# Three context k-tiles of each joint norm move from GpSimd to VectorE, and norm operations increment their readers' semaphores themselves

## The reference, cut to what matters

```python
def rms_norm_2(x, w):
    xf = x.astype(jnp.float32)
    y = xf * lax.rsqrt(jnp.mean(xf * xf, axis=-1, keepdims=True) + NORM_EPS)
    return (y * w.astype(jnp.float32)).astype(x.dtype)

def modulate(h, shift, scale):
    return h * (1.0 + scale) + shift
```

## Time and profile before

| | |
|---|---|
| median of 3 runs | 3286.22 us (3282.61 to 3289.34) |
| profiled execution, its time | 3286.13 us |
| its span, first to last instruction | 3284.1 us |
| PE busy | 3086.7 us (94%), 19874 matmuls |
| DVE busy | 1655.5 us (50%), 2636 instructions |
| ACT busy | 1155.5 us (35%), 1824 instructions |
| POOL busy | 574.0 us (17%), 500 instructions |
| mean granted TensorE clock | 0.976 |

### The profile page before, as it was taken

One profiled execution on the slowest core, in us unless ns is written; L12 is line 12 of the kernel. 1 busy time (PEld: TensorE's weight loads), 2 busy tenths in 40 slices (PEclk: granted clock), 3 DMA queues, 4 the chain that ended last, 5 costly groups with the idle time before them and its releaser, 6 DMA issues. The chain is left out here.

```text
span 3284.1 us, 49467 instructions
## 1 busy us (share of the span) xinstructions
PE 3086.7 (94%) x19874; PEld 2476.7 (75%) x19874; DVE 1655.5 (50%) x2636; ACT 1155.5 (35%) x1824; POOL 574.0 (17%) x500
## 2 busy tenths in 40 slices
PE   7988999999989999998988899999989999899998
PEld 5666766877657888776777788888868888678886
DVE  5643587455246664335663332332367877643332
ACT  4211354543123222344774311111254544432221
POOL 0000022011023441141552200000043233100000
PEclk9999999999989999998999999999989999899999
DMA  3466111223312222301000102112131121122222
GB/s 136 174 250 260 58 74 64 77 77 127 117 38 92 78 103 89 111 14 65 2 2 27 52 33 97 52 39 90 34 109 59 59 78 59 70 91 77 103 89 79
DMA packets 34146, 271.00 MB, mean 83 GB/s; under 512 B 3200, under 2 KB 5760, under 8 KB 14720
## 3 DMA queue, kind: packets, MB, share of 16 engines
q1 hardware_dynamic: 33920, 267.85, 22.6%
HBM read 263.64 MB, written 4.19 MB: 82 GB/s over the span
## 5 line engine op out<-in xcount | busy, mean ns | idle before, releaser
L751 PE MATMUL banks<-normed_high,weights_high 128*128 128x512 f32 (+1 forms) x2168 | 802.3, 378 | 27.7 <-DVEq L544 9.1
L751 PE MATMUL banks<-normed_low,weights_high 128*128 128x512 f32 (+1 forms) x2168 | 789.7, 373 | 0.0
L418 ACT ACTIVATE weights_high<-ring 128x1024 fp32r<-128x1024 f32 (+2 forms) x335 | 339.8, 1014 | 1010.4 <-PE banks L751 762.8
L308 DVE TENSOR_TENSOR weights_low<-ring,weights_high 128x1024 fp32r<-128x1024 f32 (+2 forms) x281 | 329.0, 1171 | 724.0 <-ACTq L420 706.9
L751 PEld LDWEIGHTS banks<-normed_high,weights_high 128*128 128x128 f32 x2168 | 411.8, 190 | 118.4 <-issue 17.3
L751 PE MATMUL banks<-normed_high,weights_low 128*128 128x512 f32 (+1 forms) x2168 | 497.9, 371 | 1.4 <-DVEq L440 1.4
L751 PEld LDWEIGHTS banks<-normed_low,weights_high 128*128 128x128 f32 x2168 | 411.7, 190 | 78.6 <-issue 4.6
L751 PEld LDWEIGHTS banks<-normed_high,weights_low 128*128 128x128 f32 x2168 | 380.9, 189 | 77.8 <-DVEq L440 2.3
L685 POOL TENSOR_TENSOR latent_total<-latent_total,latent_square 128x512 f32<-128x512 f32 x42 | 62.6, 1491 | 1185.3 <-ACTq L664 1185.3
L751 PE MATMUL banks<-ffn_hidden_high,weights_high 128*128 128x512 f32 (+1 forms) x704 | 251.3, 366 | 0.0
L751 PE MATMUL banks<-ffn_hidden_low,weights_high 128*128 128x512 f32 (+1 forms) x704 | 251.1, 366 | 0.0
(11 more groups left out here) (618 smaller groups left out, 4835.6 us busy)
## 6 DMA issues: line engine op xcount, KB each, us to landing
ring<-in_ada SPq DMA_DIRECT2D x48, 1024.0 KB, 6.4
ring<-in_ffn_up SPq DMA_DIRECT2D x22, 2048.0 KB, 8.1
ring<-in_hgrn SPq DMA_DIRECT2D x16, 1536.0 KB, 6.3
ring<-in_ffn_down SPq DMA_DIRECT2D x16, 1408.0 KB, 6.0
ring<-in_gates SPq DMA_DIRECT2D x6, 2048.0 KB, 8.1
ring<-in_wo SPq DMA_DIRECT2D x6, 2048.0 KB, 8.1
ring<-in_ffn_up2a SPq DMA_DIRECT2D x4, 2048.0 KB, 8.1
ring<-in_ffn_up2b SPq DMA_DIRECT2D x4, 2048.0 KB, 8.0
```

Source lines behind the costliest of these rows:

```text
L308: e.eng.tensor_tensor(out, x, hi.bitcast(F32), ALU.subtract).then_inc(e.sem, e.tick())
L418: e.eng.activation(self.by_k(k.WH), self.source(), ACT.Copy).then_inc(e.sem, e.tick())
L751: mm = pe.matmul(ps[:, 0:y.shape[-1]], w, y, start=(kk == 0 and n == 0), stop=(kk == kt - 1 and n == len(every) - 1))
```

## The change

The context norms of `q2`, `ffn_up2a` and `hgrn` get `rest=5` and a `partner`, the latent norm of the same place. GpSimd makes context k-tiles 0 to 4. VectorE makes 5 to 7 in a new loop, `by_rest`, behind its latent norm, in the partner's `scaled` buffers, with two operations a k-tile; ScalarE's roundings keep their order. PE waits for them through `wait_ready`. Norm operations now increment their reader's semaphore themselves; the waits for the engine's own counter and the separate increments are gone, except one inside GpSimd between L540 and L308. `scaled` has three buffers where there is room (`w_rw`, `wk`, `ffn_up2a`, `hgrn`), with a wait for the low part that last read the buffer. In `ffn_up`, `ffn_up3` and `q2` it stays at two. The unsplit norms and `Rounded` are changed alike. In `hgrn`, `clear_keys` waits for five context k-tiles of GpSimd instead of eight.

```diff
@@ class Normed
+    def wait_ready(self, eng, t):
+        c, n = self.ready_at(t)
+        eng.wait_ge(c.sem, c.at(n + 1))
...
     def by_scalar_rounding(self, e, t):
+        if t >= self.rest:
+            n = t - self.rest
+            x = self.partner.scaled[n % len(self.partner.scaled)][:, 0:self.width]
+            e.eng.wait_ge(self.rest_made.sem, self.rest_made.at(n + 1))
+            e.eng.activation(self.dst(t)[0], x, ACT.Identity, bias=self.shift(t)).then_inc(self.rest_rounded.sem, 1)
+            return
...
-            e.eng.activation(hi, x, ACT.Identity, bias=self.shift(t), scale=gain).then_inc(e.sem, e.tick())
-        e.eng.wait_ge(e.sem, e.now())
-        e.eng.sem_inc(self.rounded.sem, 1)
+            e.eng.activation(hi, x, ACT.Identity, bias=self.shift(t), scale=gain).then_inc(self.rounded.sem, 1)
+
+    def by_rest(self, e):
+
+        v, left, depth = e.eng, DT - self.rest, len(self.partner.scaled)
+        v.wait_ge(self.rooted.sem, self.rooted.at(1))
+        for n in range(left + 1):
+            if n >= depth and n < left:
+                v.wait_ge(self.rest_ready.sem, self.rest_ready.at(n - depth + 1))
+            if n < left:
+                t = self.rest + n
+                v.scalar_tensor_tensor(self.partner.scaled[n % depth][:, 0:self.width], self.src(t), self.gain(t), self.root,
+                                       ALU.mult, ALU.mult).then_inc(self.rest_made.sem, 1)
+            if n:
+                t = self.rest + n - 1
+                hi, lo = self.dst(t)
+                v.wait_ge(self.rest_rounded.sem, self.rest_rounded.at(n))
+                v.scalar_tensor_tensor(lo, self.partner.scaled[(n - 1) % depth][:, 0:self.width], self.shift(t), hi.bitcast(F32),
+                                       ALU.add, ALU.subtract).then_inc(self.rest_ready.sem, 1)
...
-        for t in range(DT + 1):
-            if t < DT:
-                scale(t, self.scaled[t % 2])
-                eng.sem_inc(self.made.sem, 1)
+        depth = len(self.scaled)
+        for t in range(self.rest + 1):
+            if t < self.rest:
+                if t >= depth:
+                    eng.wait_ge(self.ready.sem, self.ready.at(t - depth + 1))
+                scale(t, self.scaled[t % depth], self.made)
...
                 elif self.on == "vector":
-                    eng.scalar_tensor_tensor(lo, x, self.shift(t - 1), hi.bitcast(F32), ALU.add, ALU.subtract).then_inc(e.sem, e.tick())
+                    eng.scalar_tensor_tensor(lo, x, self.shift(t - 1), hi.bitcast(F32), ALU.add, ALU.subtract).then_inc(self.ready.sem, 1)
...
-                eng.wait_ge(e.sem, e.now())
-                eng.sem_inc(self.ready.sem, 1)
@@ linear, vector
                 for n, r in enumerate(mine):
                     r.by_scaler(e, first_weights if n == 0 else None)
+                for r in norms:
+                    if r.rest < DT:
+                        r.by_rest(e)
```

More of the change, by code:

```diff
@@ L303, in operand, with low_part_for @@
         return lambda kk: self.at(kk, cols)
+def low_part_for(e, out, x, hi, ready):
+    e.eng.tensor_tensor(out, x, hi.bitcast(F32), ALU.subtract).then_inc(ready.sem, 1)
 def low_part(e, out, x, hi):
@@ L464, in __init__ @@
     def __init__(self, name, src, width, bank, gain, dst, shift=None, on="vector", part=0, eps=NORM_EPS,
-                 behind=None, root=None, scaled=None):
+                 behind=None, root=None, scaled=None, depth=3, rest=DT,
+                 partner=None):
+        self.depth, self.rest, self.partner = depth, rest, partner
         self.name, self.src, self.width, self.bank, self.gain, self.dst = name, src, width, bank, gain, dst
@@ L474, in place, with ready_at @@
         if self.split and self.scaled is None:
-            buf = k.sb(self.name + "_scaled", [P, 2, self.width], stack)
-            self.scaled = [buf[:, b, :] for b in range(2)]
+            buf = k.sb(self.name + "_scaled", [P, self.depth, self.width], stack)
+            self.scaled = [buf[:, b, :] for b in range(self.depth)]
         self.rooted, self.made, self.rounded, self.ready = (k.count(f"{self.name}_{x}") for x in (
             "rooted", "scaled", "rounded", "normed"))
+        if self.rest < DT:
+            self.rest_made, self.rest_rounded, self.rest_ready = (k.count(f"{self.name}_rest_{x}") for x in (
+                "scaled", "rounded", "normed"))
+    def ready_at(self, t):
+        return (self.rest_ready, t - self.rest) if t >= self.rest else (self.ready, t)
+    def wait_ready(self, eng, t):
+        c, n = self.ready_at(t)
+        eng.wait_ge(c.sem, c.at(n + 1))
     def ends(self, ends):
         ends[self.rooted_name()] = 1
-        ends[self.name + "_normed"] = DT
+        ends[self.name + "_normed"] = self.rest
         if self.split:
-            ends[self.name + "_scaled"] = ends[self.name + "_rounded"] = DT
+            ends[self.name + "_scaled"] = ends[self.name + "_rounded"] = self.rest
+        if self.rest < DT:
+            for x in ("scaled", "rounded", "normed"):
+                ends[f"{self.name}_rest_{x}"] = DT - self.rest
     def rooted_name(self):
@@ L541, in by_scaler @@
                     eng.wait_ge(e.sem, e.now())
-                    low_part(e, lo, x, hi)
-                eng.wait_ge(e.sem, e.now())
-                eng.sem_inc(self.ready.sem, 1)
+                    low_part_for(e, lo, x, hi, self.ready)
+        eng.wait_ge(self.ready.sem, self.ready.at(self.rest))
 class Rounded:
@@ L553, in __init__, with wait_ready @@
         self.rounded, self.ready = k.count(name + "_rounded"), k.count(name + "_parted")
+    rest = DT
     def place(self, k, stack):
         pass
+    def wait_ready(self, eng, t):
+        eng.wait_ge(self.ready.sem, self.ready.at(t + 1))
     def ends(self, ends):
@@ L706, in _ @@
                         for kk in range(kt):
[L707 removed]
+                            gates[part].wait_ready(pe, kk)
                             hi, lo = parts[part](kk)
@@ L1136, in rwkv_inputs @@
         N = k.sb("rw_norms", [P, MT, L], s)
-        lead = norm_of(root=N[:, 0, :], scaled=[N[:, 1, :], N[:, 2, :]])
+        lead = norm_of(root=N[:, 0, :], scaled=[N[:, x, :] for x in range(1, MT)])
         def shift(e, n, part, ps, at_):
@@ L3260, in hgrn @@
         flat = SS[:].rearrange("p a c n -> p (a c n)")
-        latent = norm_of(1, root=AT[:].rearrange("p c n -> p (c n)"), scaled=[SQ[:], A2[:].rearrange("p c n -> p (c n)")])
-        context = norm_of(0, root=flat[:, 0:CTX], scaled=[flat[:, CTX:2 * CTX], flat[:, 2 * CTX:3 * CTX]])
+        latent = norm_of(1, root=AT[:].rearrange("p c n -> p (c n)"), scaled=[SQ[:], A2[:].rearrange("p c n -> p (c n)"), QH[:].rearrange("p d c n -> p (d c n)")])
+        context = norm_of(0, rest=5, partner=latent, root=flat[:, 0:CTX], scaled=[flat[:, x * CTX:(x + 1) * CTX] for x in range(1, 4)])
         norms = (latent, context)
@@ L3349, in project_pair @@
                         for kk in range(DT):
-                            pe.wait_ge(norms[part].ready.sem, norms[part].ready.at(kk + 1))
+                            norms[part].wait_ready(pe, kk)
                             hi, lo = H.at(kk, c)
@@ L3585, in clear_keys @@
                     v.wait_ge(n["residual_parked"].sem, n["residual_parked"].at(16))
-                    v.wait_ge(context.ready.sem, context.ready.at(DT))
+                    v.wait_ge(context.ready.sem, context.ready.at(context.rest))
                     v.memset(KI[:], 0.0).then_inc(e.sem, e.tick())
@@ L3719, in _ @@
                 latent.by_scaler(e)
+                context.by_rest(e)
                 lower_bounds()
```

42 lines of the change are left out of this document (21 added, 21 removed).

## The result

| | before | after |
|---|---|---|
| median | 3285.8 us (3282.6 to 3289.3, 6 runs) | 3260.4 us (3257.2 to 3262.6, 6 runs) |
| profiled execution, its span | 3286.13, 3284.1 us | 3257.16, 3255.4 us |
| mean granted TensorE clock | 0.976 | 0.981 |

The ratio is 0.9921, with a 95% interval of 0.9909 to 0.9934: 25.4 us between the medians. The forecast was 3265.5 with a range from 3261.5, so the kernel is faster by 5 us more than forecast and lies 1.1 us under the range.

The account below looks back on a forecast made before the run. PE was taken to stand behind the norms. Increments 5.7 us, latent stretches 2.4 + 2.6 + 2.0 and context stretches 2.5 + 2.5 + 3.0 sum to 20.7: 3286.2 - 20.7 = 3265.5 us, range 3261.5 to 3276.5.

Parts of the forecast that it names:

- The bound: Whole kernel: PE, busy for 94% of the span, stands behind the norms at the norm stages, k-tile by k-tile.
- Increments outside the joint norms: `w_rw` 2.5 us, memory norm 0.4, `wk` 2.0, `ffn_up`, `ffn_up3` and `wo3` 0.75; sum 5.7 us (4.0 to 7.0).
- the 1.25 end of the bounds: In `w_rw` a latent k-tile falls from 1.73 us to between 1.25 and 1.49; 1.35 was taken.
- The size of the memory norm: Memory norm: eight operations last 4.91 us, without gaps 3.3.
- The rule of the Trainium skill: VectorE chaining without semaphores saves nothing: only separate increments saved, `w_rw` k-tile 1.49 us, whole sum about 18 us, 3268.
- Latent stretches: `q2`, `ffn_up2a`, `hgrn`: without gaps 1.62 us a k-tile, PE the bound or nearly; gains 2.4, 2.6 and 2.0 us.
- the 1.80 that was given as the most: Latent k-tile in the joint norms if every VectorE operation is stretched to 0.99 us: 1.80 us.
- Rival A: Joint norms: VectorE and GpSimd contention stretches both; latent gains nothing, contexts 1.5 us each; 10.2 us in all, 3276; 14%.
- Context stretches: `q2`, `ffn_up2a`, `hgrn`: moving three k-tiles from GpSimd to VectorE gains 2.5, 2.5 and 3.0 us; low end 1.0 each.
- Rival B: ScalarE's k-tile 5 queues behind GpSimd's k-tile 4; each context stretch loses 1 to 1.5 us of gain; 3269 to 3270; 14%.
- Rival C: VectorE and GpSimd operations wait each other out wholly; costs 5 us a joint place; slower, 3295 us; 4%.
- starts from the pair's last matmul and moves with it: Work behind each pair, weights rounded and DMAs issued on PE's counts, shifts with the pair's end; no term in the sum.

Follow-up runs that it names:

- before_again: The kernel before, unchanged, run once more for a second profile; 3284.5 us in its one run.
- move_only: Changed kernel with own waits and separate increments back in every norm operation, `rest=5` kept; ratio 0.9949 to the kernel before, 16.8 us.
- rest0: Changed kernel with VectorE taking all eight context k-tiles behind the latent ones, GpSimd's final norm in `q2` waiting for them; 3261.1 us, 0.9918 to the kernel before.
- inc_single: Kernel before with increments without wait only in the norms that stand alone; joint norms old but for the third buffer; ratio 0.9974 to the kernel before.
- no_adjust: Changed kernel with GpSimd's TENSOR_SCALAR (gain and shift of context k-tiles) left out; 3255.4 us in its one run.

## Why the prediction missed, step by step

*The bound* was read rightly: PE behind the norms. The windows show it, not rows 1: about 19 of the 22.0 us there are waits for the first k-tile of a norm, and 18 of them are still there. The contexts' wait for GpSimd is gone, the 2.17 us in `wk` are gone, and the total followed the pairs.

*Increments outside the joint norms: 5.7 us forecast; 6.5 between the first two profiles, 7.8 over all four* (3.2 or 3.7 to the end of `w_rw`, 3.1 or 3.9 in the memory norm and `wk`, 0.2 in `ffn_up`; `wo3` and `ffn_up3` can't be told from chance). In `w_rw` the k-tile is 1.26 us, the 1.25 end of the bounds, not the 1.35 that was taken: waits whose count was reached long before cost nothing. The size of the memory norm was right (3.27 against 3.3). The larger figures hold a half-clock stretch at 814 us and, in `w_rw`, matmuls that start 0.43 us apart until 32 us instead of 23. Both are in `before_again` and also in `move_only`, which has the old norms in these places (50.0 and 81.9 us), and in no kernel with the new ones.

The rule of the Trainium skill, "VectorE: DVE Perf Modes", section "The DRAIN you can't avoid", by which chaining without semaphores saves nothing, would have left `w_rw` at 1.49 us a k-tile. The trace has 1.26. The same section also says that a next operation "that is not held starts earlier", and the trace has such an earlier start: 0.60 and 0.66 us from start to start for 0.69 and 0.75 us of work.

*Latent stretches: 7.0 us forecast, 4.4 measured.* This is the step that failed by most: "without the gaps, at those durations, 1.62 us. So PE becomes the bound, or nearly." The durations didn't stay. GpSimd's two TENSOR_TENSORs still took their turns in every two latent k-tiles. Waiting for them, which had partly lain in VectorE's gaps, moved into its operations (0.99 us became 1.22), and a k-tile took 1.88 us, past the 1.80 that was given as the most. Of the 0.96 us of gaps in two k-tiles only 0.39 were worth anything. Rival A named this, that contention eats the gain; it took 2.6 us and not all, and `rest0` shows that 2.6 us are what PE could still gain.

*Context stretches: 8.0 forecast, 9.0 measured*, 8.4 of it standing and 0.5 the clock in `hgrn` (8.98 us before, 8.47 in `inc_single`). Rival B, the rest late, didn't come: lateness begins when GpSimd makes seven k-tiles, not six.

*Rival C, exclusion.* Its time, 3295 us, didn't come, but its mechanism was there all along: the ends show the engines serving one operation at a time, in the kernel before as well. What was wrong is its price, and with it the forecast's reading that rows 7 "speak for sharing". It took the recorded 0.75 us and 2.0 us for the turns. A turn of VectorE behind GpSimd is 0.54 or 0.55 us, one of a TENSOR_TENSOR 0.59 to 0.61 and one of the TENSOR_SCALAR 0.26; with these, and 0.68 from one VectorE operation to the next, two latent k-tiles and a context one take 3.76 us, where the durations alone, 4 x 0.66 (`rest0`) + 0.73 + 0.56 + 0.73, give 4.7. The merge of rows 10 fits: it ends at 740.08, 0.54 us behind GpSimd's operation. The Trainium skill, "SBUF — State Buffer", section "SBUF: two separate sides", has the lock exclusive and held for the whole instruction. The trace agrees with the turns; they are shorter than the recorded durations. That a port is what they take turns at, no run here shows.

*What the sum left out.* The forecast said of what follows a pair that it "starts from the pair's last matmul and moves with it". In the profiles it also ran at a higher clock: 3.1 us behind the three pairs. Of this 1.9 is in `q2`, which both profiles of either kernel show, 1.2 in `ffn_up2a`, from `before_again` alone, and none in `hgrn`. That term was 0 in the forecast. Against the forecast the account reads -2.6 (latent), +1.0 (context), +2.1 (increments alone), +3.1 (clock behind the pairs) and +1.6 in stages that differ as much between two profiles of one kernel: 20.7 + 5.2 = 25.9. The terms that the forecast had priced measured 4.4 + 9.0 + 7.8 = 21.2 us, near its 20.7: a latent term too high and two others too low, which nearly cancel. What lies beyond them is the clock's 3.1 us and the 1.6. The range was missed by 1.1 us. Without the 1.9 us of clock in `q2` the time would lie inside it, and likely without the 1.6 too, so that it fell below and not just inside is in part chance. What stays open is how much of the clock in `ffn_up2a` and `hgrn` is bound to the standing, since two profiles of one kernel differ there by up to 2.3 us.

## What to carry over

Let an operation increment its reader's semaphore itself, and give its output a third buffer where the only wait left would be for the operation just ahead: in a two-operation loop on VectorE that was worth 0.47 us of 1.73, 0.12 of it the buffer. When gaps are closed on VectorE beside a busy GpSimd, don't keep the old durations: look at the order of the ends, count GpSimd's turns in VectorE's time, or see whether VectorE can do GpSimd's part in the slack. And a stall of 3 us in front of a dense stretch can cost more than itself: in `q2` and `ffn_up2a` the clock fell behind it in 7 of 8 cases, and in 4 of 18 with less standing. Look at the granted clock behind it before summing, in more than one profile.

## What the runs showed of the hardware

- VectorE's 128x512 operations start 0.60 and 0.66 us apart for 0.69 and 0.75 us of work when nothing unmet is waited for. A wait for the one just ahead adds 0.12 us (1.38 instead of 1.26 us for two), and a separate increment behind such a wait about as much again, an estimate: (1.73 - 1.26 - 2 x 0.12) / 2.
- VectorE's 128x512 two-source operations and GpSimd's 128x256 ones end one by one, in the kernel before, the changed one and `no_adjust`: VectorE's 0.54 or 0.55 us behind GpSimd's, and GpSimd's TENSOR_TENSOR 0.59 to 0.61 us behind VectorE's. Whichever starts second is stretched: VectorE's from 0.75 to 0.99 or 1.22 us, GpSimd's from 0.73 to between 0.96 and 1.26.
- A TENSOR_SCALAR of GpSimd beside VectorE lasted up to 1.49 us instead of 0.56 and let a whole VectorE operation of 0.75 us go ahead; it cost the one behind 0.13 us. It ended 0.26 us behind VectorE's operation in the changed kernel and 0.43 in the kernel before.
- The granted clock differs between executions of one kernel. Half-clock stretches in stages far from any edit moved or vanished, by up to 5 us of the chunk stage; the distance between two single profiles is no measure of a change under 5 us unless the same stretch is compared in several.
